# Half of the modulation pieces multiplied between the streams of the first block, and the second block's input norms reordered

## What is computed

```python
def second_block(...):
    xl, xc = x, ctx
    for li in range(DEPTH):
        mod_l = jnp.split((jax.nn.silu(c) @ ada_w[li] + ada_b[li])[:, None, :], 6, axis=-1)
        mod_c = jnp.split(jax.nn.silu(c_ctx) @ ada_w[li] + ada_b[li], 6, axis=-1)
        hl = rmsnorm_2(xl, norm1_g[li]) * (1.0 + mod_l[1]) + mod_l[0]
        hc = rmsnorm_2(xc, norm1_g[li]) * (1.0 + mod_c[1]) + mod_c[0]
        ...
        xl = xl + mod_l[2] * ol
        hl = rmsnorm_2(xl, norm2_g[li]) * (1.0 + mod_l[4]) + mod_l[3]
        xl = xl + mod_l[5] * sq_relu_mlp(hl, mlp_w1[li], mlp_w2[li])
        ...
```

## Time and profile before

| | |
|---|---|
| time, median of 3 runs (lowest to highest) | 3619.67 us (3615.26 to 3625.52) |
| the profiled execution's own time | 3617.66 us |
| its span, first to last instruction | 3615.5 us |
| PE busy | 3258.3 us, 90% of the span |
| PEld busy | 2787.4 us, 77% |
| DVE busy | 1895.6 us, 52% |
| ACT busy | 1405.6 us, 39% |
| POOL busy | 356.6 us, 10% |
| mean granted TensorE clock | 0.944 of full speed |
| moved by the transfers | 459.77 MB, mean 127 GB/s |

### The profile page before, as it was taken

The page is one execution under the profiler, slowest core; times in us unless marked ns, Lnnn a source line. Parts: engine busy times, 40 slices in busy tenths (PEclk is TensorE's granted clock), DMA queues, the critical chain, the costliest instruction groups (busy, mean ns, idle before and its releaser), DMA issues.

```text
span 3615.5 us, 54646 instructions
## 1 busy us (share of the span) xinstructions
PE 3258.3 (90%) x22888; PEld 2787.4 (77%) x22888; DVE 1895.6 (52%) x2581; ACT 1405.6 (39%) x2037; POOL 356.6 (10%) x387
## 2 busy tenths in 40 slices
PE   7989999898998999989898689898899979896897
PEld 7878887697887788779676578886688868786795
DVE  4356645445445664544524666663333367576554
ACT  3345554335335544433522333331323244412443
POOL 2000000100100000010010233330000001033000
PEclk9999999899999999999999789998899989987999
DMA  9655545665765555476441000002232223500464
GB/s 266 213 155 167 165 150 177 205 210 173 246 197 159 163 170 151 160 235 198 145 127 41 1 2 8 2 3 82 72 99 94 88 71 88 146 1 12 135 180 133
DMA packets 449227, 459.77 MB, mean 127 GB/s; under 512 B 18288, under 2 KB 347184, under 8 KB 449008
## 3 DMA queue, kind: packets, MB, share of 16 engines
q1 hardware_dynamic: 428624, 385.08, 35.8%
q0 software_dynamic: 20384, 71.52, 5.9%
HBM read 455.50 MB, written 1.05 MB: 126 GB/s over the span
## 4 chain that ended last, share of the span: by engine, by line
PE 75%; DVE 15%; ACT 5%; issue 4%; DMA 1%; POOL 1%; DVEq 0%; ACTq 0%; SPq 0%; POOLq 0%
PE banks L311 20%; PE banks L312 19%; PE banks L313 19%; PE banks L1901 2%; DVE weights_lo L297 1%; PE banks L4275 1%; PE banks L3518 1%; PE banks L3520 1%; PE banks L3499 1%; PE banks L1287 1%; DVE arena L3921 1%; DMA arena<-in_ada_w 1%; DVE first_input_split L1298 1%; PE banks L4246 1%; DVE arena L1430 1%
## 5 line engine op out<-in xcount | busy, mean ns | idle before, releaser
L297 DVE TENSOR_TENSOR weights_lo<-raw_weights,weights_hi 128x1024 fp32r<-128x1024 f32 (+2 forms) x399 | 472.7, 1186 | 544.7 <-ACT weights_hi L289 470.4
L289 ACT ACTIVATE weights_hi<-raw_weights 128x1024 fp32r<-128x1024 f32 (+2 forms) x399 | 409.3, 1027 | 530.5 <-PE banks L313 525.0
L262 DVE TENSOR_TENSOR weights_lo<-raw_weights,weights_hi 128x1024 fp32r<-128x1024 f32 x180 | 220.8, 1228 | 472.8 <-ACT weights_hi L255 285.2
L255 ACT ACTIVATE weights_hi<-raw_weights 128x1024 fp32r<-128x1024 f32 x180 | 190.4, 1060 | 516.9 <-PE banks L313 511.5
L311 PE MATMUL banks<-first_input_split,weights_hi 128*128 128x256 f32 (+1 forms) x1218 | 357.9, 294 | 9.1 <-DVE first_input_split L1298 5.2
L313 PE MATMUL banks<-first_input_split,weights_lo 128*128 128x256 f32 (+1 forms) x1218 | 347.9, 286 | 0.0
L312 PE MATMUL banks<-first_input_split,weights_hi 128*128 128x256 f32 (+1 forms) x1218 | 346.9, 285 | 0.0
L297 DVE TENSOR_TENSOR third_weights_split<-raw_weights,third_weights_split 128x1024 fp32r<-128x1024 f32 (+1 forms) x173 | 207.1, 1197 | 233.3 <-ACT third_weights_split L289 190.9
L311 PE MATMUL banks<-work_split,weights_hi 128*128 128x512 f32 (+2 forms) x776 | 272.2, 351 | 24.0 <-DVEq L2405 20.2
L312 PE MATMUL banks<-input_split,weights_hi 128*128 128x512 f32 (+2 forms) x776 | 270.6, 349 | 0.0
L313 PE MATMUL banks<-work_split,weights_lo 128*128 128x512 f32 (+2 forms) x776 | 270.4, 349 | 0.0
(11 more groups left out here) (597 smaller groups left out, 7169.2 us busy)
## 6 DMA issues: line engine op xcount, KB each, us to landing
raw_weights<-in_w_ffn_gu SPq DMA_DIRECT2D x176, 512.0 KB, 4.7
raw_weights<-in_w_in SPq DMA_DIRECT2D x144, 512.0 KB, 3.7
raw_weights<-in_mlp_w SPq DMA_DIRECT2D x128, 512.0 KB, 3.9
arena<-in_ada_w POOLq DMA_DIRECT2D x96, 512.0 KB, 6.7
raw_weights<-in_w_ffn_down SPq DMA_DIRECT2D x80, 512.0 KB, 3.4
raw_weights<-in_w_branch SPq DMA_DIRECT2D x48, 512.0 KB, 3.6
raw_weights<-in_ssd_w_in SPq DMA_DIRECT2D x48, 512.0 KB, 3.9
raw_weights<-in_w_mkv SPq DMA_DIRECT2D x32, 512.0 KB, 4.2
```

The lines of the kernel that those rows point to most:

```text
L255: last = s.activation(self.w_hi[:, u % 2, :], self.raw[:, u, :], ACT.Copy)
L262: last = v.tensor_tensor(self.w_lo[:, u % 2, :], self.raw[:, u, :], self.w_hi[:, u % 2, :].bitcast(F32), ALU.subtract)
L289: last = s.activation(hi, raw, ACT.Copy)
L297: last = v.tensor_tensor(lo, raw, hi.bitcast(F32), ALU.subtract)
```

## The change

The 96 pieces and the 24 groups stay, and what is computed stays. What is different:

- There are nine slots in the arena where there were five, and three or eight more places for pieces in arena rows whose contents have been read: the hidden rows of a rows stretch (`more_modulations`), and the `V_TOK`, `U_TOK` and `SV_TOK` rows of the mixing part's branches.
- Beside the feed-forward streams only 12, 12, 8 and 12 pieces are multiplied (44). `multiply_modulations` emits the other 52 between two streams, right after the last product of the one that ends: 12 after each of the first three feed-forwards that are followed by a stream of the first block, and 8 after each output projection. Their sums are taken as the first side work of the next stream.
- Pieces beside a stream are brought one per unit, nine ahead of the first product, and each transfer also waits until all units but the last few emitted are multiplied.
- `normed_input` transposes through banks 0 to 3, not 4 to 7, because banks 6 and 7 now hold the modulation sums. DVE clears the padding of the convolution after `normed_input`, not ahead of it.
- `modulated_input` splits the first two units of weights first, squares the fourth tile after the first tile's affine modulation, and makes each tile's parts after the affine modulation of the next tile. The first product of the hybrid mixer waits for each tile by itself.

```diff
 STRIP = 32
-MOD_SLOTS = 5
+MOD_SLOTS = 9
...
+            pe.wait_ge(self.steps_done, at - 1 if tiles_made else at)
...
         per_unit = KD // UNITS
+        waits = list(tiles_made or ())
         def product(banks, u, hi, lo, pe):
             for n, t in enumerate(tiles):
+                if waits:
+                    pe.wait_ge(*waits.pop(0))
                 for j in range(per_unit):
                     k, tokens = u * per_unit + j, slice(t * P, (t + 1) * P)
...
-        feature_major(c, ch, c.y[:, t, :], x, t, 4 + 2 * t)
+        feature_major(c, ch, c.y[:, t, :], x, t, 2 * t)
     stream.split_ahead(3)
...
-    mod_rows, pick = cols(z, GATES, 2, SEQ), cols(c.small, 448, 2, 2)
-    mod_slots = [cols(z, MOD_AT + n * UNIT, 2, BANK) for n in range(MOD_SLOTS)]
+    mod_rows, pick = cols(z, LD_AT + P, 3, SEQ), cols(c.small, 448, 2, 2)
...
+    def bring_modulation_weights(at, *free):
+        m = c.mods_brought
...
+        used = [piece for piece, place in c.mods_at.items() if place == at]
...
+            if used or m >= MOD_ARRIVALS:
+                g.wait_ge(c.mods_multiplied, max(used + [m - MOD_ARRIVALS]) + 1)
+            g.dma_start(cols(z, at, 2, BANK), src).then_inc(c.mods_arrived[m % MOD_ARRIVALS], 16)
+        c.mods_at[m] = at
+        c.mods_brought += 1
+    def multiply_modulation():
...
+        slot = cols(z, c.mods_at[m], 2, BANK)
+        bank, columns = 6 + area // 2, slice(area % 2 * SEQ, (area % 2 + 1) * SEQ)
...
+            pe.wait_ge(c.mods_arrived[m % MOD_ARRIVALS], 16 * (m // MOD_ARRIVALS + 1))
+            if u == 0:
+                pe.wait_ge(ch.steps_done, ch.steps)
...
+        c.mod_pieces += 1
+    def modulation_sums():
...
+        ch, first, pieces = c.side, c.mod_groups, c.mod_pieces
+        count = pieces // UNITS - first
+        c.mod_groups += count
...
+            s.wait_ge(c.mods_multiplied, pieces)
+            s.wait_ge(ch.steps_done, ch.steps)
+            for i in range(count):
+                last = s.activation(mod_rows[:, i, :], c.ps[:, 6 + i // 2, i % 2 * SEQ:(i % 2 + 1) * SEQ], ACT.Copy)
+            last.then_inc(ch.steps_done, 1)
+        yield
+        yield
...
+    def modulation_groups(beside, ahead):
+        free = [chain_end(ch) for ch in c.tile + [c.side]]
+        first, end = c.mods_brought, c.mods_brought + UNITS * beside + ahead
+        def bring_some():
+            while c.mods_brought < min(end, c.mod_pieces + MOD_SLOTS):
+                at = MOD_AT + (c.mods_brought - first) % MOD_SLOTS * UNIT
+                bring_modulation_weights(at, (c.multiplied, c.units_split - 1), *(free if at == MOD_AT else ()))
+                yield
+                yield
+        for _ in range(beside):
             for u in range(UNITS):
+                yield from bring_some()
+                multiply_modulation()
                 yield
+            yield from modulation_sums()
+        yield from bring_some()
+    def more_modulations(stream, count):
+        rows = stream.todo[-1][0]
+        for i in range(count):
+            bring_modulation_weights(i * UNIT, (c.lo_made, rows.numbers[4 * i + 3] + 1 + UNITS))
+    def multiply_modulations():
+        while c.mod_pieces < c.mods_brought:
+            multiply_modulation()
...
+        for i in range(4):
+            bring_modulation_weights(V_TOK + i * UNIT, chain_end(ch))
         yield from emitted(st["kv"])
...
+        for i in range(2):
+            bring_modulation_weights(U_TOK + i * UNIT, chain_end(ch))
         yield from emitted(st["gates"])
...
+        for i in range(2):
+            bring_modulation_weights(SV_TOK + i * UNIT, chain_end(ch))
...
-        memory = itertools.chain(memory_input(layer), params_needed() if layer == 0 else (),
-                                 modulation_columns(12 * layer, [chain_end(ch) for ch in c.tile + [c.side]]))
+        memory = itertools.chain(modulation_sums(), memory_input(layer), params_needed() if layer == 0 else (),
+                                 modulation_groups(3 - layer, MOD_SLOTS + 3))
         st, sides = {}, []
...
+        more_modulations(stream, 3)
+        multiply_modulations()
         stream = mixing
         add_normed(c, done, slots[1], 0.5)
...
+        normed_input(c, slots[2], x_in, stream)
...
         def _(v):
+            v.wait_ge(c.mods_multiplied, c.mod_pieces)
+            v.wait_ge(c.side.steps_done, c.side.steps)
             v.memset(qk_pad[:, :, 0:3], 0.0).then_inc(c.side.steps_done, 1)
...
-        normed_input(c, slots[2], x_in, stream)
...
-        side = branches(layer, st)
+        side = itertools.chain(modulation_sums(), branches(layer, st))
...
         done = run(outs, None, stream)
+        multiply_modulations()
         add_normed(c, done, slots[0], 1.0)
...
-        columns = modulation_columns(12 * layer + 6, [chain_end(ch) for ch in c.tile + [c.side]])
+        last = layer == DEPTH - 1
+        columns = itertools.chain(modulation_sums(), modulation_groups(3, 0 if last else MOD_SLOTS + 3))
...
+        if last:
             scales()
+        else:
+            more_modulations(stream, 3)
+            multiply_modulations()
...
-    try_root(c)
-    for t, ch in enumerate(chains):
...
+    def squared(t, ch):
...
-    for t, ch in enumerate(chains):
+    def normed(t, ch):
...
-    if stream:
-        stream.split_ahead(2)
-    else:
-        c.split_first_weights()
-    for t, ch in enumerate(chains):
...
+    def features(t):
+        return y[:, t, :].rearrange("p (k n) -> p k n", n=P)
+    def modulated(t, ch):
+        y_t = features(t)
...
+    def parts(t, ch):
+        tokens = slice(t * P, (t + 1) * P)
...
+    try_root(c)
+    if stream:
+        stream.split_ahead(2)
+    else:
+        c.split_first_weights()
+    first = min(tiles, 3)
+    for t in range(first):
+        squared(t, chains[t])
+    for t in range(first):
+        normed(t, chains[t])
+    modulated(0, chains[0])
+    for t in range(first, tiles):
+        squared(t, chains[t])
+        normed(t, chains[t])
+    for t in range(1, tiles):
+        modulated(t, chains[t])
+        parts(t - 1, chains[t - 1])
+    parts(tiles - 1, chains[tiles - 1])
+    c.tiles_made = chain_ends(chains)
     joined(c, chains)
     c.x_hi, c.x_lo = hi, lo
...
     c.gemm_token_major(range(ROWS), 6, column_chunks(a["hy_w_in_2"][0], 0), BANK,
-                       *token_copies(c, rows, range(ROWS)), more=True)
+                       *token_copies(c, rows, range(ROWS)), more=True, tiles_made=c.tiles_made)
```

116 lines of the change are left out of this document (47 added, 69 removed).

## The result

The changed kernel took **3563.12 us** (median of 3560.13 to 3577.59), the kernel before 3621.03 beside it: 0.9852 of it, 95% interval 0.9829 to 0.9875, so 58 us less. Measured again later it took 3557.27, 0.9815 (0.9797 to 0.9834). The median of all eight executions is 3560.5. I forecast 3538, 0.977 of the kernel before, with 3563 as the upper end; the first measurement lies just above it. The direction was right, and the gain is 16 to 24 us short of the forecast. Two single executions further on, one of the kernel before (5428.52 us) and one of the kernel with the sums twice (15981.99 us), lay far off all others and are left out everywhere.

What follows compares the result with a forecast made beforehand. PE was taken to bound the feed-forward streams, ACT and DVE the intervals between and the second block's input norms. Terms 40.0 + 12.8 + 5 + 6 + 17.6 = 81.4 us off 3617.66 gave 3536.3, forecast 3538; range 3521 to 3563.

Steps and rivals of the forecast that it cites:

- Pieces, 40.0 us: Streams that PE bounds: 52 of 96 pieces leave, at 0.77 us each, 40.0 us less PE work.
- the intervals at cost 0: Between streams: the moved pieces fit under DVE's and ACT's chain of add and norm, so they cost nothing.
- first waits and their clock: Start of feed-forward streams: 12.8 us of waits for first pieces, plus 5 us for the clock lowered by that idling.
- The rival of intervals that don't hold them: Between streams: PE at half clock, twelve pieces last 12.1 us, transposes come late; 3560 us, chance 0.12.
- First-piece waits, 12.8 us: Beside each feed-forward: PE finds its first piece already landed, so the whole 12.8 us goes; lower bound about 8.
- That rival's 3562: Stream starts: transfers starve the weights, four streams lose 6 us, first-piece waits and their clock stay; 3562 us, chance 0.06.
- the lag of 1.5 us: While nine pieces are brought: nine units take 27.6, not 26.1 us, a lag that four raw buffers absorb.
- The clock behind each interval, 6 us: After five first-block intervals: pieces in the idle time keep the clock higher; 6 us gained, bounds 0 and 12.5.
- Norms, 17.6 us: Second block's four input norms and the hybrid mixer's start: new order fills waits; 17.6 us, between 8 and 20.
- The term for the second norm, 4.7: Second call of the input norm: same shape as the first, so also 4.7 us.
- the signs that I had named for a wrong forecast: Piece over 0.6 us between streams, transposes released by PE, ACT waiting for raw weights early, clock behind intervals as low.
- Its lower end, 3521: Whole kernel: the range's lower end, said to have every term at its better bound.

Runs made afterwards that it cites:

- the sums twice: The changed kernel with each set of pending sums (13 groups) multiplied twice in a row at the start of the stream; 3586.56 us, ratio 0.9903.
- both edits: Changed kernel with pending sums emitted 5 to 7 units later and three, not two, steps between piece transfers beside a stream; 3546.21 us, again 3545.94.
- The dense matmuls: Kernel with both edits plus 20 full-size, unread matmuls behind each interval's pieces: 3540.42 us, again 3538.37; the same added to the changed kernel alone: 3554.51.

## Why the prediction was wrong, and what in it held

**Pieces, 40.0 us, and the intervals at cost 0: right.** With both edits the streams are shorter by what was booked (58.1 and 54.0 us against 57.8, first waits and their clock included), and in the changed kernel the first transposes come 7.8, 7.5, 8.6, 8.1 and 7.5 us behind the last product (before: 7.8, 7.5, 8.6, 7.8, 7.5). Only the fourth is 0.3 us later. The rival of intervals that don't hold them is out: twelve pieces take 5.39 us, not 6.8 and not 12.1.

**First-piece waits, 12.8 us: the waits went, part of the gain was paid back.** I gave the transfers one sentence of cover and a chance of 0.06, and tied the rival to first-piece waits that stay. They went, yet the first half of that rival came: PE loses 4.7 us in the first feed-forward and some 3 in the second layer's first. That rival's 3562 is close to the number that came out, but that is luck: 17.8 of its 24 us are first waits and their clock, which didn't come. The step that failed here is the lag of 1.5 us that four raw buffers absorb. It measured 3 to 5 us in the first feed-forward (184.3 to 186.5 us against 181.5), which PE did lose.

**The clock behind each interval, 6 us: wrong in sign.** This was the step that failed most. It counted pieces and transposes and left out the sums, which the change moves to the first side work of the next stream. The mechanism held inside the intervals, where pieces now stand: the low clock there fell from 44.7 us to 19.0 and 12.6, but PE waits there anyway. Behind the intervals, where it costs, it didn't shrink from 27.1 us but grew to 41.3 and 38.5. At half of each us lost, that is 6 or 7 us worse than before and 12 or 13 worse than booked, and outside the bounds of 0 and 12.5 that I had given. With both edits it is 15.5 and 21.3 (18.9 and 24.7 over 30 us), which gives back 1 to 6 us of the 6 booked. The Trainium skill, "TensorE: Matmul & The Clock Gate", section "Part 1: The HAM clock gate (the "warmup" mystery)", says that activity of the array lifts the clock. By the rule as I read it, a PE at work keeps the upper level. The traces don't agree with that reading: PE is busy for 13.99 of 14.00 us at a clock of 0.64, and for the 5.11 us of the sums it works without a gap at the lower level.

**Norms, 17.6 us: right mechanism, 14 by the times, 16.2 by the trace.** The term for the second norm, 4.7, measured 2.2. I gave it the shape of the first and overlooked that POOL works there: DVE's two low parts take 4.70 us beside it and not 2.36.

**What would show it.** Of the signs that I had named for a wrong forecast, two came: ACT waiting for raw weights early in a stream, and a clock behind an interval as low as before (0.64 against 0.80 over 14 us). Both pointed at the cause.

**The range.** Its lower end, 3521, doesn't follow from the terms: with each at its better bound (clock 6 and 12.5 us, norms 20) the sum is 91.3 us and the time 3528.

**The rest.** Of the 22.5 us between the forecast and the eight executions, the two edits give back 14.6 and the norms explain 1.4 (by the trace) to 3.6 (by the times). The dense matmuls bring the kernel to 3538.37, which is the forecast by number, not by mechanism: the forecast had the clock rise with the pieces alone. What stays open is the last 4 to 6.5 us. They may be lower clock inside streams, which comes and goes between executions of one kernel; no run separates that.

## What to carry over

Work that is moved has followers: list every small step that goes with it, and where in the next stretch it lands. Here small matmuls were cheaper in the middle of dense products (2.73 us for 24 passes, and half the time a stretch of 3.4 us at the lower clock behind them) than at the start of a stream (5.11 us, in a stretch of 10). Judge a prefetch by the gaps of PE behind it, and not by those of the loading engine alone. And where an engine's work is moved, look at what the other engines do at its new place: the same instruction took 1.23 us beside an idle POOL and up to 2.92 beside a busy one.

## What I had not expected of the hardware

- A pass of two moving columns took 0.21 us behind an interval and 2.73 / 24 = 0.11 us in the middle of a stream (the row below is of the kernel with both edits). With 24 of them behind the first interval PE is busy throughout, and the clock stays at its lower level.

```profile
255.49 2.73 PE L1932 MATMUL banks<-small,arena 128*128 128x2 f32 x24
```

- The four matmuls of a piece, on four strips of 32 columns, take 5.39 / 12 = 0.45 us together; with one of the four left in nine of twelve pieces, the twelve take 5.37. Strips run side by side here, and leaving three out saves nothing.
- 20 dense matmuls in 2.66 us, behind the pieces, kept the upper level through all five intervals of three traces (0.8 us at the lower at most), though PE still waits about 2 us there for the first product.
- DVE's low part of a unit of weights took 1.23 us with POOL idle, 1.86 and 2.92 us beside two operations of POOL on arrays of the same size (thirteen traces).
